# The order of turns, queries and scores in TensorE's item list of a hybrid decoder layer with expert retrieval

## What is computed

```python
merged = g_conv * conv_y + g_swa * (swa_o @ w_swa_out) + g_mem * (mem_o @ w_mem_out)
x = x + merged @ w_out
x = x + peer_ffn(rmsnorm(x, norm2_g), peer_w_q, peer_keys, peer_w_down, peer_w_up)
...
q = (xb @ w_q).reshape(PEER_BLOCK, PEER_HEADS, 2, PEER_DK_HALF)
s = jnp.einsum('thcd,hcnd->thcn', q, keys, preferred_element_type=jnp.float32)
sv, si = lax.top_k(s, PEER_TOPK)
...
u = w_down[eid]
act = jax.nn.gelu(jnp.einsum('td,thkd->thk', xb, u, preferred_element_type=jnp.float32), approximate=False)
return jnp.einsum('thk,thkd->td', (gate * act).astype(xb.dtype), w_up[eid])
```

## Time and profile before

| | |
|---|---|
| median of 3 runs | 3350.51 us (3348.85 to 3361.31) |
| the profiled execution | 3348.85 us, span 3347.1 us |
| TensorE matmul busy | 3087.0 us (92%) |
| VectorE busy | 2512.8 us (75%) |
| GpSimd busy | 1611.7 us (48%) |
| ScalarE busy | 779.2 us (23%) |
| moved by DMA | 1077.16 MB, 322 GB/s over the span |
| row gathers (q0) | 625.03 MB, 48.7% of 16 engines' span |
| loads by SyncE (q1) | 428.87 MB, 34.1% |

### The profile page before, as it was taken

One profiled execution on the slowest core, in us unless ns is written; L12 is line 12 of the kernel. 1 busy time (PEld: TensorE's weight loads), 2 busy tenths in 40 slices (PEclk: granted clock), 3 DMA queues, 4 the chain that ended last, 5 costly groups with the idle time before them and its releaser, 6 DMA issues.

```text
span 3347.1 us, 33154 instructions
## 1 busy us (share of the span) xinstructions
PE 3087.0 (92%) x11349; PEld 1818.7 (54%) x11349; DVE 2512.8 (75%) x5082; ACT 779.2 (23%) x2063; POOL 1611.7 (48%) x1269
## 2 busy tenths in 40 slices
PE   8999798998989999779999999999999999997874
PEld 5677687866847654445545445545545545543321
DVE  2298434986889789888988888888888868455556
ACT  2001542321310114324214204204204214200000
POOL 0000002545145677745566667557657657444434
PEclk9999899999998999899999999999999999998998
DMA  3111466999599999999999999999999999899998
GB/s 130 43 37 58 147 204 231 336 334 354 197 339 351 359 404 397 331 368 370 381 353 388 357 380 388 344 389 385 358 377 380 359 400 373 335 410 393 408 410 316
DMA packets 326171, 1077.16 MB, mean 322 GB/s; under 512 B 40468, under 2 KB 73877, under 8 KB 325340
## 3 DMA queue, kind: packets, MB, share of 16 engines
q0 software_dynamic: 172416, 625.03, 48.7%
q1 hardware_dynamic: 119275, 428.87, 34.1%
q10 hardware_dynamic: 34312, 21.16, 2.0%
HBM read 1052.50 MB, written 23.94 MB: 322 GB/s over the span
## 4 chain that ended last, share of the span: by engine, by line
PE 29%; DMA 20%; DVE 15%; issue 13%; POOL 10%; ACT 1%; ACTq 1%; DVEq 0%; POOLq 0%
PE psum L1666 17%; DMA arena<-in_w_down,arena 12%; POOL arena L1404 9%; DMA arena<-in_w_up,arena 7%; DVE arena L2019 5%; PE psum L1469 4%; PE psum L1642 2%; PE psum L1529 2%; PE psum L1513 1%; ACTq L2264 1%; PE psum L1612 1%; DVE arena L2113 1%; DMA arena<-scratch_s 1%; DMA arena<-in_w_q 1%; PE psum L1515 1%
## 5 line engine op out<-in xcount | busy, mean ns | idle before, releaser
L1404 POOL DMA_INDIRECT arena<-in_w_down,arena x1024 | 1419.2, 1386 | 735.5 <-DVE arena L2019 503.1
L1666 PE MATMUL psum<-arena 128*128 128x512 f32 x3584 | 1602.0, 598 | 77.1 <-DMA arena<-in_w_up 70.8
L2019 DVE CUSTOM_DVE_ANT_0 arena<-arena 128x1024 f32<-128x1024 f32 x1024 | 1220.0, 1222 | 256.3 <-DMA arena<-in_w_down,arena 247.8
L1666 PEld LDWEIGHTS psum<-arena 128*128 128x128 f32 x3584 | 664.4, 191 | 871.0 <-issue 734.3
L1513 PE MATMUL psum<-arena 128*128 128x256 f32 (+2 forms) x1536 | 361.6, 390 | 17.0 <-DVEq L1831 5.5
L2321 ACT ACTIVATE arena<-arena 128x128 f32<-128x128 f32 x896 | 285.6, 390 | 323.8 <-DVE arena L2043 314.7
L2043 DVE TENSOR_TENSOR arena<-constants,arena 128x1024 f32<-128x1024 f32 x224 | 273.4, 1224 | 77.7 <-PE psum L1469 65.0
L1513 PEld LDWEIGHTS psum<-arena 128*128 128x128 f32 x1536 | 267.9, 195 | 99.5 <-issue 13.3
L1469 PEld LDWEIGHTS psum<-arena 128*128 128x128 f32 x1792 | 237.8, 195 | 153.2 <-ACT arena L2321 86.6
L1469 PE MATMUL psum<-arena 128*128 128x128 f32 x1792 | 245.0, 281 | 40.4 <-ACT arena L2321 40.2
L2113 DVE SCALAR_TENSOR_TENSOR arena<-arena 128x1024 f32<-128x1024 f32 x128 | 164.4, 1284 | 122.6 <-DMA arena<-in_w_up,arena 121.3
(11 more groups left out here) (317 smaller groups left out, 2039.8 us busy)
## 6 DMA issues: line engine op xcount, KB each, us to landing
arena<-in_w_up SPq DMA_DIRECT2D x512, 512.0 KB
arena<-in_w_gates SPq DMA_DIRECT2D x96, 768.0 KB
arena<-in_w_o SPq DMA_DIRECT2D x40, 512.0 KB
arena<-in_w_q SPq DMA_DIRECT2D x32, 512.0 KB
arena<-in_w_down,arena POOLq DMA_INDIRECT x1024
arena<-in_w_chunks SPq DMA_DIRECT2D x26, 512.0 KB, 3.5
arena<-scratch_s POOLq DMA_DIRECT2D x64, 128.0 KB
scratch_s<-arena ACTq DMA_DIRECT2D x11, 512.0 KB
```

Of the source, the lines that this page charges most:

```text
L1404: pool.indirect_dma_start(dst, None, table, bass.IndirectOffsetOnAxis(ap=idN[:, min(n, NT - 1) % 2, j:j + 1], axis=0)).then_inc(here, 16)
L1666: mm = pe.matmul(psum[:, 2 * (m % 2) + h, :], coef_block(m, s % NKEYS), wup[s % WUPR][:, h * 512:(h + 1) * 512], start=first, stop=end)
L2019: dve.tensor_tensor_reduce(row, row, rowD[slot_of["x", n]], 1.0, 0.0, ALU.mult, ALU.add, dots[:, n % 3, j:j + 1]).then_inc(row_used, 1)
```

## The change

The items themselves stay the same; their order changes in group 2 (tiles 3 and 4, whose pairs carry the turns and queries of tiles 1 and 2) and in group 3 (whose pairs carry those of tiles 3 and 4). In group 2 both turns stand together behind two pairs, the four queries stand in a row behind one more pair, the scores follow at once, and attention step 18 comes behind them; the attention steps go every second pair to step 26, with one pair left behind the last. In group 3 the turns of tiles 3 and 4 come before `xs`, the four queries stand in a row, `xt` and `xv` come with one pair between them, and the scores follow `xv`.

```diff
         pr = pairs_of(2, 0)
-        qs = queries(1)
-        items += pr[0:2] + outs(1, 0) + pr[2:3] + att(18) + pr[3:5] + turns([1]) + pr[5:6] + turns([2]) + qs[0:1] + pr[6:7] + qs[1:2]
-        items += pr[7:8] + qs[2:3] + pairs_of(2, 1, 2)[0:1] + qs[3:4] + scores([1, 2])
-        items += mixed(pairs_of(2, 1, 2)[1:], range(19, NU + 2), 2) + att(NU + 2)
+        items += pr[0:2] + outs(1, 0) + pr[2:4] + turns([1, 2]) + pr[4:5] + queries(1) + scores([1, 2])
+        items += mixed(pr[5:] + pairs_of(2, 1, 2), range(18, NU + 3), 2)
         pr = pairs_of(3, 0)
-        qs = queries(2)
-        items += pr[0:1] + outs(2, 0) + pr[1:2] + [("xs",)] + turns([3, 4]) + pr[2:3] + qs[0:1] + pr[3:4] + qs[1:2] + [("xt",)]
-        items += pr[4:5] + qs[2:3] + [("xv",)] + qs[3:4] + scores([3, 4]) + pr[5:] + pairs_of(3, 1, 2)[0:12] + [("ids0",)] + pairs_of(3, 1, 2)[12:]
+        items += pr[0:1] + outs(2, 0) + pr[1:2] + turns([3, 4]) + [("xs",)] + pr[2:3] + queries(2) + [("xt",)] + pr[3:4] + [("xv",)]
+        items += scores([3, 4]) + pr[4:] + pairs_of(3, 1, 2)[0:12] + [("ids0",)] + pairs_of(3, 1, 2)[12:]
```

## The result

The changed kernel takes 3381.05 us (median of 6 runs, 3371.71 to 3392.07), the kernel before 3348.44 us in the same comparison: ratio 1.0099, 95% interval 1.0077 to 1.0122. It is slower, and outside the range of the prediction (up to 3374). The profiled execution took 3405.39 us with a span of 3403.6; before, the span was 3347.1, so the two profiles differ by 56.5 us where the medians differ by 33. The profiles show where the time goes; how much it is, the ratios tell. The changed kernel's profile is of its slowest execution. Lines of the changed kernel are 3 lower than those of before: L1639 is a query, L1619 a turn, L1510 and L1512 a pair, L1401 a row fetch.

The account below looks back on a forecast made before the run. Row fetches held at rows 122 and 184, then full DMA engines from 1100 us, were taken to bound the kernel. "xv" shifting -2 us and row 184 following sooner, -3, gave -5: forecast 3346 us, range 3326 to 3374.

Parts of the forecast that it names:

- What bounds the kernel: Full DMA engines from 1100 us; before, row fetches stop at row 122 (last attention item) and row 184 ("xv" copy).
- Part 1, the queries in a row: Group 2: four queries at 8.8 us each, 35.2 instead of 41.0; net -5.8 us, bounds -12.5 and 0.
- Part 1, the turns: Group 2: a slot wait of 4.2 us goes, the second turn waits 2 us (bounds 0 and 21); net -2 us.
- Part 1, attention and evacuations: Group 2, attention steps and remaining pairs: some evacuations come late because of tile 1's selections; +3 us, bounds 0 and 12.
- Part 2, the last attention step earlier: End of group 2: row 122 may go 5.2 us sooner, worth nothing because of 25 us of slack before row 184.
- Part 3, the turns of group 3: Turn 4 waits 1.6 us (bounds 0 and 12.8), the first query's 2.9 us wait goes; net -1.3 us.
- Part 3, the queries before "xv": Group 3: four queries, 35.2 us, replace three queries and a pair, 30.6; +4.6 us, bounds -0.7 and +10.6.
- Part 4, row 184 behind its copy: After "xv": row 184 follows the copy sooner, filling up to 7.8 us; worth 3 us, bounds -3 and 0.
- Rival A: Groups 2 and 3: turns wait for late norms, 15 us or more and 12.8 us; 3370 us, chance 0.20.
- Rival B: Groups 2 and 3: queries don't wait, -12.5 and -0.7 us instead of -5.8 and +4.6; 3334 us, chance 0.18.
- Rivals C and D: C: tile 1's rows fill the first hole, 3305 us, chance 0.04; D: gates hold, nothing moves, 3350 us, chance 0.08.
- The rule beside the rows: Weights got 119 GB/s beside row fetches; equal queue turns would give 185: either the queue lacks work or turns are unequal.

Follow-up runs that it names:

- closing the second hole: Kernel before with "xt" and "xv" ahead of group 3's queries, which removes the row fetches' pause from 1075 to 1100 us: 3348.06 us, ratio 0.9973.
- The release at half: Changed kernel, but a query's first ring buffer is released when the query's first half is done, not at its end: 3353.38 us, ratio 1.0012.
- both edits: Changed kernel with a query's first buffer released at its half, group 2's turns behind three pairs, "xs" before group 3's turns: 3344.68 us, ratio 0.9967.
- the early release on the old order: Kernel before, with a query's first buffer released when its first half is done: 3339.05 us, ratio 0.9962.
- the square: Changed kernel, ratio by turns and query release: neither edited 1.0099, turns later 1.0045, first buffer released at half 1.0012, both 0.9967.
- first edit: Changed kernel with only the turns moved, group 2's behind three pairs and group 3's behind "xs": 3363.87 us, ratio 1.0045.
- group 2 and 3 alone: Kernel before with the new order in one group only: group 2 3355.29 us, ratio 1.0018; group 3 3371.04 us, ratio 1.0051.

## Why the prediction was wrong, point by point

Three of its own signs of being wrong came: waits of over 5 us at both pairs of turns (11.6 and 15.4), queries of over 10 us (three of the four in group 2), and row 184 after 1110 (at 1137).

- **What bounds the kernel: right.** What had not been moved by 1100 was moved later at the pace of the full engines; of the MB missing by 1320 (20.5 when summed by stretch), 0.7 fell before 721, 4.5 between 721 and 1100 (292 GB/s against 304), 9.4 between 1100 and 1140 (147 against 383) and 5.9 to 1320. But "the stream's position is fixed by the two gates" says too much: closing the second hole is worth 0.27% alone and nothing where the queries are released early. TensorE's own position counts beside the gate's; in the changed list both slip together.
- **Part 1, the queries in a row: the step that failed.** It took 119 GB/s for the weights' own pace and 8.8 us for a query. Measured: 12.3, 12.9 and 13.6 us behind the first, 45.4 in all instead of 35.2 (neighbours overlap by some 0.2 us in the profile). The upper bound, 4 x 10.3 = 41.2, failed too. It named the right mechanism (both ring buffers released only at a query's end), but priced it with the waits of the earlier trace rows, which stand behind pairs. A pair between two queries hides 5.2 us of the load; without it the whole 7.3 us load stands behind each query but for the half query beside it. The rest, some 6 us in all, is the slower clock (0.83). The release at half puts the queries back to 7.1 to 7.9 us.
- **Part 1, the turns: too small.** 11.6 us of waits instead of 2 (4.8, 5.4 and 7.1 in the profiles of three other kernels with the same pairs and turns). VectorE's list of the changed kernel has five dot products and an evacuation between the two norms, and two of them wait for their rows:

```profile
732.62 1.28 DVE L1850 SCALAR_TENSOR_TENSOR arena<-arena,constants 128x1024 f32<-128x1024 f32 x1
...
738.78 1.23 DVE L2016 CUSTOM_DVE_ANT_0 arena<-arena 128x1024 f32<-128x1024 f32 x1 [1.11 <-DMA arena<-in_w_down,arena]
...
741.73 1.23 DVE L2016 CUSTOM_DVE_ANT_0 arena<-arena 128x1024 f32<-128x1024 f32 x1 [1.71 <-DMA arena<-in_w_down,arena]
...
743.07 1.28 DVE L1850 SCALAR_TENSOR_TENSOR arena<-arena,constants 128x1024 f32<-128x1024 f32 x1
```

- **Part 1, attention and evacuations: about right.** +3, bounds 0 and 12. The outs of group 2 ended 18.6 us later (988.3 against 969.7). The turns account for 11.6 - 4.2 = 7.4 of it, the slower pair behind them for 1.7, the queries for 45.4 - 41.0 = 4.4, which leaves 5. The largest single wait in this remainder is the 6.2 us of an attention step for VectorE.
- **Part 2, the last attention step earlier: right.** Row 122 went later with the group (955 against 940), and the 62 rows behind it were issued 46 us before gate 184 opened. The slack did not run out.
- **Part 3, the turns of group 3: the other step that failed.** 10.4 + 5.0 = 15.4 us instead of 1.6. The argument was that tile 1's selections would be done by then. They were not: the scores came 13 us sooner, not 35, and the last selection of tile 1 and the first of tile 2 still stood before the add, which began 13.2 us behind the outs (11.5 before):

```profile
991.09 0.29 DVE L1895 MAX8 arena<-arena 128x8 f32<-128x128 f32 x1
...
1000.28 1.23 DVE L2016 CUSTOM_DVE_ANT_0 arena<-arena 128x1024 f32<-128x1024 f32 x1
...
1001.43 2.36 DVE L1838 TENSOR_TENSOR arena<-arena,psum 128x1024 f32<-128x1024 f32 x2
```

  "xs", which had stood in front of the turns and covered this, now stood behind them. Moving it back costs one line and gives 1.0051 to 1.0013.
- **Part 3, the queries before "xv":** +8.6 us instead of +4.6 (39.2 against 30.6), inside the bound of +10.6. The four took 7.1, 12.3, 7.6 and 12.5 us. "xv" thus shifted by 18.6 + 15.4 - 2.9 + 8.6 = 39.7 by these terms, 43.8 measured (the start of its matmuls, 1101.1 against 1057.3); 4 us stay without a term.
- **Part 4, row 184 behind its copy: right** (0.3 us). Whether it was worth the 3 us that it was given can't be seen among the 44.
- **The rivals.** Rival A (the turns wait) was right in mechanism at both places and said 3370; its 15 and 12.8 us were 9.4 and 5.0 at the second turns, 11.6 and 15.4 with the first. It is about half: the turns are 0.45 to 0.54% of time. The other half is the queries, for which the prediction had no rival on the slow side, only a bound. Rival A was given 0.20; the release at a query's end should have had a chance of its own. Rival B (the queries don't wait, 3334) is the run with the early release as to the queries, and even that stands at 1.0012 while the turns wait. Rivals C and D did not happen.
- **The rule beside the rows.** Four queries at 7.1 to 7.9 us take 1.05 MB each, about 144 GB/s beside the rows, with the same list and only an earlier release. So the 119 GB/s of the kernel before was not the share that the weights' queue was granted; the queue had nothing to do for part of the time: in the kernel before it moved nothing from 758 to 766.6, while the first query ran. The Trainium skill, "DMA: Bandwidth & Descriptors", section "Queues, rings and completion order", speaks of queues that have work. Where both have work the trace comes near equal turns: from 765 to 768 the changed kernel moved 156 packets of weights and 183 of rows, and from 1157 to 1162, with no weights asked for, 495 packets of the scores' writes and 495 of rows. The 144 of 395 GB/s is an average over a stretch in which TensorE asked for no more. Of the two readings left open in the prediction the first ("the queue has not always work") was the right one, and the sum should have asked what empties it.

In sum, the new order of group 2 and 3 gains nothing with both edits: 0.9967, against 0.9962 for the early release on the old order. The 0.99% is, by the square, 0.54% for the turns (first edit), 0.40% for what the release then cures in the new list beyond what it cures in the old (0.78 - 0.38), and 0.05% that is left; taken in the other order 0.45, 0.49 and 0.05. Each is good to about 0.3%. Shown by experiments are these two. Only read from the profiles is why VectorE's list puts the norms late; that group 2 and 3 alone add to 0.69% and not 0.99% is within the intervals and left open. Open, too, is why the release gives the old order twice what its queries had waited.

## What to carry to other kernels

Before items of one kind are put in a row, look at what refills their buffers: a wait measured between two items with other work between them is only what that work did not hide, and the price in a row is the whole load less what of it can be issued ahead. Where a multi-buffer item releases all of its buffers at its end, releasing each when it has been read is a small edit and was worth 0.38% here without any change of order. And a long item that needs nothing from the late engine ("xs", 27 us) belongs in front of the item that does.

## What the runs showed of the hardware

- Behind the scores of tiles 3 and 4 TensorE ran in fragments of one to five matmuls with idle times of 0.2 to 1.6 us that end at nothing the profile shows, from 1148 to 1167 in the changed kernel, about 12 us in all; the weight loads in front of the matmuls have the same gaps.

```profile
1150.80 0.49 PE L1512 MATMUL psum<-arena 128*128 128x392 f32 x1 [1.58 <-issue]
1152.20 1.18 PE L1512 MATMUL psum<-arena 128*128 128x392 f32 x2 [0.91 <-issue]
```

  The DMA engines were full in that time (share 1.01 from 1137 to 1180). The Trainium skill, "Runtime: NRT & Kernel Launch", section "Instruction fetch mechanics", says that an engine's instructions are fetched by DMA in blocks while it runs, mostly hidden; a fetch that queues behind full engines could look like this, but the trace doesn't bear it out: the two instruction queues (q8, q14) moved no packet at all from 1145 to 1175. The cause is open.
- The scores' writes go out in small packets: from 1137 to 1170 the queue of ScalarE moved 1.50 MB in 2976 packets and took 15.0% of the 16 engines' time, 10.0% per MB; the loads of weights moved 0.93 MB in 168 packets for 7.8%, 8.4% per MB. So a MB of writes costs only 1.2 times as much, in spite of packets of 0.5 KB. Between its copies of the scores ScalarE stood idle for up to 9.0 us, which ended at "remote"; that it waited for its own writes is likely and not shown.

```profile
q10 hardware_dynamic: 2976, 1.50, 15.0%
q1 hardware_dynamic: 168, 0.93, 7.8%
```

- While "xv" runs (matmuls with one column) the granted clock is 0.50 from 1109 to 1136, the lower of the two levels, with TensorE busy throughout.
